# Seven half-size products in place of eight for 18 of 22 gate and up pairs of a SwiGLU layer

## Chip, cores and metric

The kernel runs on one core of one Trainium2 chip. The metric is the device time of one execution in microseconds; for a version it is the median of its runs. The profile is one more execution, taken by the hardware profiler.

## The reference, cut to what matters

```
x = x + 0.5 * swiglu(rms_norm(x), gate1, up1, down1)
x = x + mixer(rms_norm(x))        # GLA, differential attention, short convolution
x = x + 0.5 * swiglu(rms_norm(x), gate2, up2, down2)
return rms_norm(x)
swiglu(h, Wg, Wu, Wd) = (silu(h @ Wg) * (h @ Wu)) @ Wd
```

x is 512 tokens by 1024, in float32. Wg and Wu are 1024 by 2816, Wd is 2816 by 1024. The change touches the two SwiGLU layers only.

## The kernel before

**Numbers in two parts.** Every large product is made of float32 operands that are split in two: a high part rounded to the matmul type fp32r (ScalarE, an ACTIVATE Copy) and the rest (VectorE, a subtraction). `three` (L384) issues three matmuls for one 128 by 128 block of weights: high·high, high weights by low x, low weights by high x. The weights are the stationary operand, the tokens the moving one, so one matmul has 512 columns.

**Slabs.** Weights come in slabs of 128 by 1024 (down: 128 by 1408), numbered through the whole kernel. SyncE loads slab s into `raw[slot s % 2]` when the slab before the last has been split (`load`, L276). `split_hi` (L795, ScalarE) writes `w_hi` once TensorE has used the slab two before (`slab_used`), `split_lo` (L1088, VectorE) writes `w_lo` and counts `lo_ready`, on which TensorE waits (`wait_slab`, L381).

**Up stage** (`ffn_up`, L447 on TensorE, L845 on ScalarE, L1122 on VectorE). 22 pairs, each a gate tile and an up tile of 128 of the 2816 columns: 8 blocks deep, so 24 matmuls of 512 columns for the gate tile, 24 for the up tile. For each pair VectorE scales the gate tile out of PSUM by the inverse norm (L1146), then the up tile (L1150), ScalarE takes silu (L868), VectorE multiplies (L1155), ScalarE makes `h_hi` (L872), VectorE `h_lo` (L1157). In between, both engines split the next slabs. Each engine works its list strictly in the order written.

**Down stage** (`ffn_down`, L479, L885, L1175). Eight output tiles, each 22 blocks deep, two slabs a tile, 66 matmuls of 512 columns; VectorE adds the tile to x (L1172), and the split operand of the next stage is made from it (L807, L1100). GpSimd sums the squares of x for the next norm (L332, L334). In the second layer the last tile is computed in two token halves with matmuls of 256 columns (`last_tile`, L522), so that the final norm of the first half runs beside the second half.

**Start.** The first pair runs as its weights arrive in pieces; the norm of the first layer is ready during the second pair (`mean_squares`, `spread_rms`). Then TensorE makes small products for the mixer (`start_products`, L393) and VectorE their copies (`start`, L1249).

Of the kernel before, what the change touches and what calls it, by code (L numbers as in the profile page):

```python
# [117 lines left out]
def slab_width(s):  # L118

    if s < DN1 or WO <= s < DN2:  # L120
        return UPW
# [1502 lines left out]
```

## Time and profile before

| what | value |
|---|---|
| median of 3 runs | 1024.68 us (1023.26 to 1025.01) |
| the profiled execution, its own time | 1024.96 us |
| its span, first to last instruction | 1023.0 us |
| granted TensorE clock, mean share of full | 0.988 |
| TensorE busy | 1002.9 us of the span (98%) |
| VectorE busy | 500.9 us (49%) |
| ScalarE busy | 356.3 us (35%) |
| GpSimd busy | 73.4 us (7%) |

A matmul's record is longer than the distance to the next one, because matmuls overlap in the array; what a matmul costs in a stream is the distance between two starts. The waits listed with an instruction are the idle time of its engine just before it and the instruction that ended it. A stretch row gives the busy time of each engine between two times.

### The profile page before, as it was taken

Reading aid. Unit: us, or ns where it says so; the run is one execution under the profiler, and the core shown is the slowest. Engines: PE = TensorE matmul, PEld = TensorE weight load, DVE = VectorE, ACT = ScalarE, POOL = GpSimd, SP = SyncE. Lnnn points to the kernel's source line nnn. Section 1 sums busy time; section 2 is a strip of 40 time slices with the busy share of each in tenths; the row PEclk is TensorE's granted clock in tenths of the full one; section 3 lists DMA queues with packets and bytes.
Section 4 is the critical chain, followed back from the end, with each engine's and each line's share of the span. In section 5 each row is a group of like instructions: output and inputs, shape, how many; then the busy total and the mean of one; then the engine's idle time right before and its main releaser. Section 6 shows DMA issues by size and latency. Waiting matters only on the chain.

```text
span 1023.0 us, 13402 instructions
## 1 busy us (share of the span) xinstructions
PE 1002.9 (98%) x5064; PEld 835.2 (82%) x5064; DVE 500.9 (49%) x732; ACT 356.3 (35%) x485; POOL 73.4 (7%) x76
## 2 busy tenths in 40 slices
PE   9999999999999999999989999999999999999996
PEld 8788888888888888777878788888888888888886
DVE  6444444444343433866656874444444444523233
ACT  5444334433321213445723233332332332322231
POOL 0000000000021232000112004300000000000002
PEclk9899999999999999999989999999999999999998
DMA  6222322222323224112211112223222223332312
GB/s 196 87 97 96 103 96 89 103 103 97 113 85 113 85 85 151 63 62 68 71 37 63 63 66 99 92 94 103 84 101 103 89 95 103 113 106 85 113 57 82
DMA packets 28321, 94.89 MB, mean 93 GB/s; under 512 B 3856, under 2 KB 7088, under 8 KB 28288
## 3 DMA queue, kind: packets, MB, share of 16 engines
q1 hardware_dynamic: 26096, 90.98, 26.6%
q0 software_dynamic: 896, 2.39, 0.8%
q10 hardware_dynamic: 1296, 1.07, 0.3%
q8 instruction: 22, 0.36, 0.2%
q14 instruction: 11, 0.09, 0.0%
HBM read 92.00 MB, written 2.42 MB: 92 GB/s over the span
## 4 chain that ended last, share of the span: by engine, by line
PE 45%; DVE 3%; ACT 1%; issue 1%; POOL 0%; DVEq 0%; POOLq 0%
PE ps L386 14%; PE ps L387 14%; PE ps L388 14%; DVE x L1227 1%; PE ps L635 1%; DVE e_dec L1335 1%; DVE a_comp L1355 1%; ACT w_hi L803 0%; PE ps L667 0%; PE ps L675 0%; PE ps L605 0%; DVE w_lo L1094 0%; DVE states L1381 0%; PE ps L511 0%; DVE e_dec L1362 0%
## 5 line engine op out<-in xcount | busy, mean ns | idle before, releaser
L386 PE MATMUL ps<-xg_hi,w_hi 128*128 128x512 f32 x840 | 332.2, 395 | 3.0 <-DVE w_lo L1094 2.1
L387 PE MATMUL ps<-xg_lo,w_hi 128*128 128x512 f32 x840 | 328.5, 391 | 0.0
L388 PE MATMUL ps<-xg_hi,w_lo 128*128 128x512 f32 x840 | 328.5, 391 | 0.0
L803 ACT ACTIVATE w_hi<-raw 128x1024 fp32r<-128x1024 f32 (+2 forms) x153 | 172.6, 1128 | 434.7 <-PE ps L388 434.6
L1094 DVE TENSOR_TENSOR w_lo<-raw,w_hi 128x1024 fp32r<-128x1024 f32 (+2 forms) x153 | 204.0, 1334 | 181.1 <-ACT w_hi L803 181.0
L386 PEld LDWEIGHTS ps<-xg_hi,w_hi 128*128 128x128 f32 x840 | 158.7, 189 | 44.4 <-issue 8.7
L388 PEld LDWEIGHTS ps<-xg_hi,w_lo 128*128 128x128 f32 x840 | 158.5, 189 | 33.5
L387 PEld LDWEIGHTS ps<-xg_lo,w_hi 128*128 128x128 f32 x840 | 158.8, 189 | 32.0
L386 PE MATMUL ps<-h_hi,w_hi 128*128 128x512 f32 (+1 forms) x374 | 141.0, 377 | 0.0
L387 PE MATMUL ps<-h_lo,w_hi 128*128 128x512 f32 (+1 forms) x374 | 140.8, 377 | 0.0
L388 PE MATMUL ps<-h_hi,w_lo 128*128 128x512 f32 (+1 forms) x374 | 140.8, 377 | 0.0
L1150 DVE TENSOR_TENSOR up_s<-ps,rinv 128x512 f32<-128x512 f32 x44 | 30.4, 691 | 112.7 <-PE ps L388 112.7
L388 PEld LDWEIGHTS ps<-h_hi,w_lo 128*128 128x128 f32 x374 | 70.4, 188 | 13.0
L387 PEld LDWEIGHTS ps<-h_lo,w_hi 128*128 128x128 f32 x374 | 70.4, 188 | 12.8
L386 PEld LDWEIGHTS ps<-h_hi,w_hi 128*128 128x128 f32 x374 | 70.4, 188 | 12.8
L872 ACT ACTIVATE h_hi<-up_s 128x512 f32 (+1 forms) x44 | 27.8, 632 | 85.4 <-DVE up_s L1155 85.4
L1146 DVE TENSOR_TENSOR gate_s<-ps,rinv 128x512 f32<-128x512 f32 x44 | 30.4, 691 | 41.5 <-PE ps L388 38.5
L1157 DVE TENSOR_TENSOR h_lo<-up_s,h_hi 128x512 f32 (+1 forms) x44 | 30.5, 692 | 38.8 <-ACT h_hi L872 38.8
L1172 DVE SCALAR_TENSOR_TENSOR x<-ps,x 128x512 f32 (+1 forms) x23 | 15.8, 688 | 67.6 <-PE ps L388 67.6
L1100 DVE SCALAR_TENSOR_TENSOR xg_lo<-x,gain,xg_hi 128x512 fp32r<-128x512 f32 (+1 forms) x24 | 26.0, 1092 | 15.7 <-ACT xg_hi L807 15.7
L386 PE MATMUL ps<-w_hi,xg_hi 128*128 128x384 f32 x96 | 33.2, 346 | 0.0
L387 PE MATMUL ps<-w_lo,xg_hi 128*128 128x384 f32 x96 | 32.7, 341 | 0.0
(188 smaller groups left out, 802.7 us busy)
## 6 DMA issues: line engine op xcount, KB each, us to landing
raw<-up_w SPq DMA_DIRECT2D x86, 512.0 KB, 3.2
raw<-down_w SPq DMA_DIRECT2D x32, 704.0 KB, 4.0
raw<-t_w SPq DMA_DIRECT2D x18, 512.0 KB, 3.2
raw<-out_w SPq DMA_DIRECT2D x8, 512.0 KB, 3.2
raw<-nat_w SPq DMA_DIRECT2D x6, 576.0 KB, 3.8
x<-xT SPq DMA_DIRECT2D x8, 256.0 KB, 6.1
out<-x SPq DMA_DIRECT2D x8, 256.0 KB, 2.2
raw<-nat_w SPq DMA_DIRECT2D x3, 384.0 KB, 3.2
```

What stands on the lines that cost most here:

```text
L386: pe.matmul(out_ap, a[0], b[0], start=first, stop=False)
L387: pe.matmul(out_ap, a[0], b[1], start=False, stop=False)
L388: return pe.matmul(out_ap, a[1], b[0], start=False, stop=last)
L635: last = pe.matmul(ps[c * CHUNK:(c + 1) * CHUNK, bank + hd, col + b * CHUNK:col + (b + 1) * CHUNK], a, bb, start=True, stop=True)
L803: act.activation(w_hi[:, slot(s), 0:w], raw[:, slot(s), 0:w], ACT.Copy).then_inc(hi_ready, 1)
L872: act.activation(h_hi[:, m, :], up_s[:, b, :], ACT.Copy).then_inc(h_hi_ready, 1)
L1094: dve.tensor_tensor(w_lo[:, slot(s), 0:w], raw[:, slot(s), 0:w], w_hi[:, slot(s), 0:w], ALU.subtract).then_inc(lo_ready, 1)
L1100: dve.scalar_tensor_tensor(xg_lo[:, k, :], x[:, k, :], gain[:, gi, bass.ds(k, 1)], xg_hi[:, k, :], ALU.mult, ALU.subtract).then_inc(xg_lo_ ...
L1146: dve.tensor_tensor(gate_s[:, b, :], ps[:, b, :], rinv[:], ALU.mult).then_inc(gate_scaled, 1)
L1150: dve.tensor_tensor(up_s[:, b, :], ps[:, 2 + b, :], rinv[:], ALU.mult).then_inc(up_scaled, 1)
L1157: dve.tensor_tensor(h_lo[:, m, :], up_s[:, b, :], h_hi[:, m, :], ALU.subtract)\
L1172: dve.scalar_tensor_tensor(x[:, k, :], ps[:, bank, :], scale, x[:, k, :], ALU.mult, ALU.add)\
```

## The change

Of the 22 pairs of each layer the first four (`PLAIN`) stay as they are. The other 18 (`FAST`) are called units here. A unit is a product of [weights: two halves of the depth × (gate, up)] with [x: two halves of the depth × two halves of the tokens]. It is computed by Winograd's form of Strassen's scheme: seven products M1 to M7 of half the depth (4 blocks) and 256 tokens, each 4 × 3 = 12 matmuls of 256 columns, in place of eight such quarters (48 matmuls of 512 columns).

- The products need sums of the operands. Those of x (S1 to S4) are made once a layer, during the plain pairs: `a1` on ScalarE, `s_operands` on VectorE, then the split `s_hi` and `s_lo`.
- Those of the weights (T1 to T4) are made for every unit: T1 and T3 on GpSimd (`sums`), T2 and T4 on VectorE (`t2`, `t4`); they and the up slab's second half (U2) are split in three groups, GA = T1, T2; GB = T3; GC = T4, U2. Only the gate slab is still split as a slab; the up slab goes to a buffer of its own, `raw_u`.
- Results are combined on the way out of PSUM: `take` copies a partial sum to `snap` on ScalarE, and c11, c21, c12, c22 on VectorE make the four quarters (256 columns each). Banks A, B and C exist twice.
- The up tile is no longer scaled by the norm; `tile` in the down stage scales the result instead (two instructions for one), `last_half` likewise.
- h is kept in float32 and split into `h_hi` and `h_lo` in the down stage (`split_h`), where the tiles are now computed in pairs with 22 slabs of 1024 columns in place of 16 of 1408.
- The small start products move: `start_lambda` behind pair 2, `start_bias` behind unit 1, `start` behind unit 1 on VectorE. GpSimd's sums stand in its queue ahead of the store of the bias table.

The core of the diff, in the order SyncE, GpSimd, TensorE, ScalarE, VectorE. i and b number the units, v = 2i + b; f is the layer.

```diff
+def load_unit(f, up0, b, i):
+    v = 2 * i + b
+    s = up0 + 2 * PLAIN + b
+    load(s, up_w[f, v + PLAIN, 0], 2 * i)
+    if isinstance(i, int) and i == 0:
+        sp.wait_ge(slab_used, up0 + 2)
+    else:
+        sp.wait_ge(gc_lo, v + (FAST * f - 1))
+    sp.dma_start(raw_u[:, b, :], up_w[f, v + PLAIN, 1]).then_inc(u_loaded[b], 16)
...
+def sums(f, up0, b, i):
+    v = 2 * i + b
+    s = up0 + 2 * PLAIN + b
+    pool.wait_ge(raw_loaded[slot(s)], 16 * i + loads(s))
+    pool.wait_ge(u_loaded[b], 16 * i + 16 * (FAST // 2 * f + 1))
+    if not (isinstance(i, int) and v + f == 0):
+        pool.wait_ge(ga_lo, v + FAST * f)
+    pool.tensor_tensor(t_raw[:, T1, :], raw[:, slot(s), 0:HW], raw_u[:, b, 0:HW], ALU.add)\
+        .then_inc(t1_ready, 1)
+    if not (isinstance(i, int) and v + f == 0):
+        pool.wait_ge(gb_lo, v + FAST * f)
+    pool.tensor_tensor(t_raw[:, T3, :], raw_u[:, b, 0:HW], raw_u[:, b, HW:UPW], ALU.add)\
+        .then_inc(t3_ready, 1)
...
+    def blocks(bank, moving, hi, lo, first):
+        for j in range(HK):
+            c = slice(j * P, (j + 1) * P)
+            end = three(ps[:, bank, 0:HALF], (hi[:, c], lo[:, c]), moving[j],
+                        first and j == 0, j == HK - 1, not first)
+        return end
...
+    def m1_m2(i, b):
+        v = 2 * i + b
+        s = up0 + 2 * PLAIN + b
+        g_hi, g_lo = w_hi[:, slot(s), :], w_lo[:, slot(s), :]
+        if isinstance(i, int) and i == 0:
+            pe.wait_ge(gate_scaled, PLAIN * f + PLAIN - 1 + b)
+        else:
+            pe.wait_ge(c21_scaled, v + (FAST * f - 1))
+        wait_slab(s, 2 * i)
+        blocks(A_BANK[b], x_block(0, 0), g_hi[:, 0:HW], g_lo[:, 0:HW], True).then_inc(m1_done, 1)
+        if not (isinstance(i, int) and i == 0):
+            pe.wait_ge(c11_added, v + (FAST * f - 1))
+        blocks(C_BANK[b], x_block(HK, 0), g_hi[:, HW:UPW], g_lo[:, HW:UPW], True)\
+            .then_inc(slab_used, 1)
+    def m4_m3(i, b):
+        v = 2 * i + b
+        pe.wait_ge(gc_lo, v + (FAST * f + 1))
+        pe.wait_ge(snap_ready[2], v + (FAST * f + 1))
+        blocks(A_BANK[b], x_block(HK, 1), sum_hi[:, T4, :], sum_lo[:, T4, :], False)\
+            .then_inc(m4_done, 1)
+        pe.wait_ge(c22_done, v + (FAST * f + 1))
+        blocks(B_BANK[b], s_block(S4), sum_hi[:, U2, :], sum_lo[:, U2, :], False)\
+            .then_inc(m3_done, 1)
+    def m6_m5_m7(i, b):
+        v = 2 * i + b
+        if isinstance(i, int) and v == 0:
+            pe.wait_ge(s_lo_ready, HK * (f + 1))
+        pe.wait_ge(ga_lo, v + (FAST * f + 1))
+        pe.wait_ge(snap_ready[0], v + (FAST * f + 1))
+        blocks(A_BANK[b], s_block(S2), sum_hi[:, T2, :], sum_lo[:, T2, :], False)\
+            .then_inc(m6_done, 1)
+        if isinstance(i, int) and i == 0:
+            pe.wait_ge(h_ready, FT * f + PLAIN - 1 + b)
+        else:
+            pe.wait_ge(c12_done, v + (FAST * f - 1))
+        blocks(B_BANK[b], s_block(S1), sum_hi[:, T1, :], sum_lo[:, T1, :], True)\
+            .then_inc(m5_done, 1)
+        pe.wait_ge(gb_lo, v + (FAST * f + 1))
+        pe.wait_ge(snap_ready[1], v + (FAST * f + 1))
+        blocks(A_BANK[b], s_block(S3), sum_hi[:, T3, :], sum_lo[:, T3, :], False)\
+            .then_inc(m7_done, 1)
...
+    for m in range(1, PLAIN):
+        pair(m)
+        if f == 0 and m == 2:
+            start_lambda()
+    m1_m2(0, 0)
+    m6_m5_m7(0, 0)
+    m1_m2(0, 1)
+    m4_m3(0, 0)
+    m6_m5_m7(0, 1)
     if f == 0:
-        start_products()
-    with pe.Fori(1, FT // 2) as i:
-        for b in range(2):
-            pair(i, b)
+        start_bias()
+    with pe.Fori(1, FAST // 2) as i:
+        m1_m2(i, 0)
+        m4_m3(i - 1, 1)
+        m6_m5_m7(i, 0)
+        m1_m2(i, 1)
+        m4_m3(i, 0)
+        m6_m5_m7(i, 1)
+    m4_m3(FAST // 2 - 1, 1)
...
+        for i, (m, kk) in enumerate(down_tiles(d)):
+            if q == 0 and m == 0:
+                pe.wait_ge(h_lo_ready, FT * f + kk + 1)
+            last = three(ps[:, DOWN_BANKS[q % 2][m % 2], :], part(dn0 + d, i * P, (i + 1) * P),
+                         (h_hi[kk], h_lo[:, kk, :]), kk == 0, kk == FT - 1)
...
+        if m == 0:
+            for j in range(HK):
+                act.activation(a1[:, j, :], x[:, j, :], ACT.Copy, scale=gain[:, gi, j:j + 1])\
+                    .then_inc(a1_ready, 1)
+        if m == 1:
+            act.wait_ge(s_made, HK * (f + 1))
+            for j in range(HK):
+                act.activation(s_hi[:, j, :, :], s_raw[:, j, :, :], ACT.Copy).then_inc(s_hi_ready, 1)
+        if m == PLAIN - 1:
+            ga(0, 0)
+            gb(0, 0)
...
+    def take(q, i, b, bank, done, used):
+        v = 2 * i + b
+        act.wait_ge(done, v + (FAST * f + 1))
+        if not (isinstance(i, int) and v + f == 0):
+            act.wait_ge(used, v + FAST * f)
+        act.activation(snap[:, q, :], ps[:, bank[b], 0:HALF], ACT.Copy).then_inc(snap_ready[q], 1)
+    def silu(i, b):
+        v = 2 * i + b
+        act.wait_ge(c11_scaled, v + (FAST * f + 1))
+        act.wait_ge(c21_scaled, v + (FAST * f + 1))
...
+    def unit(i, b, prev):
+        v = 2 * i + b
+        s = up0 + 2 * PLAIN + b
+        if prev:
+            take(2, *prev, A_BANK, m7_done, c22_done)
+            gb(i, b)
+        take(0, i, b, A_BANK, m1_done, c11_added)
+        if prev and isinstance(i, int) and v == FAST - 1:
+            split_hi(s + 2 * i + 1)
+        else:
+            split_hi(s + 1, 2 * i)
+        if prev:
+            silu(*prev)
+            act.wait_ge(m3_done, v + FAST * f)
+        act.wait_ge(t4_ready, v + (FAST * f + 1))
+        act.activation(sum_hi[:, GC, :], raw_u[:, b, :].rearrange("p (a c) -> p a c", a=2), ACT.Copy)\
+            .then_inc(gc_hi, 1)
+        take(1, i, b, A_BANK, m6_done, c12_done)
+        if not (isinstance(i, int) and v == FAST - 1):
+            ga(*((i, 1) if b == 0 else (i + 1, 0)))
...
+    def s_operands():
+        for j in range(HK):
+            dve.wait_ge(a1_ready, HK * f + j + 1)
+            dve.scalar_tensor_tensor(s_raw[:, j, S1, :], x[:, HK + j, HALF:S], gain[:, gi, HK + j:HK + j + 1],
+                                     a1[:, j, HALF:S], ALU.mult, ALU.subtract).then_inc(s_diff, 1)
+        dve.tensor_tensor(s_raw[:, :, S3, :], a1[:, :, 0:HALF], a1[:, :, HALF:S], ALU.subtract)
+        dve.wait_ge(s_diff, (HK + 1) * f + HK)
+        dve.scalar_tensor_tensor(s_raw[:, :, S2, :], s_raw[:, :, S1, :], -1.0, a1[:, :, 0:HALF],
+                                 ALU.mult, ALU.subtract).then_inc(s_diff, 1)
+        dve.wait_ge(s_diff, (HK + 1) * (f + 1))
+        for j in range(HK):
+            dve.scalar_tensor_tensor(s_raw[:, j, S4, :], x[:, HK + j, 0:HALF],
+                                     neg_gain[:, gi, HK + j:HK + j + 1], s_raw[:, j, S2, :],
+                                     ALU.mult, ALU.subtract).then_inc(s_made, 1)
...
+        if m == PLAIN - 1:
+            t2(0, 0)
+            t4(0, 0)
+        if m:
+            split_lo(s + 2)
+        if m == PLAIN - 1:
+            ga(0, 0)
+            gb(0, 0)
+        dve.wait_ge(slab_used, s + 2)
+        dve.wait_ge(silu_done, FT * f + m + 1)
+        dve.tensor_tensor(h[:, m, :], gate_s[:, b, :], ps[:, 2 + b, :], ALU.mult).then_inc(h_ready, 1)
+        if m and m < PLAIN - 1:
+            split_lo(s + 3)
+        if m == 1:
+            s_operands()
+        if m == 2:
+            for j in range(HK):
+                dve.wait_ge(s_hi_ready, HK * f + j + 1)
+                dve.tensor_tensor(s_lo[:, j, :, :], s_raw[:, j, :, :], s_hi[:, j, :, :], ALU.subtract)\
+                    .then_inc(s_lo_ready, 1)
+    def t2(i, b):
+        v = 2 * i + b
+        dve.wait_ge(t1_ready, v + (FAST * f + 1))
+        dve.tensor_tensor(t_raw[:, T2, :], t_raw[:, T1, :], raw_u[:, b, HW:UPW], ALU.add)\
+            .then_inc(t2_ready, 1)
+    def t4(i, b):
+        v = 2 * i + b
+        dve.wait_ge(t3_ready, v + (FAST * f + 1))
+        dve.wait_ge(t2_ready, v + (FAST * f + 1))
+        dve.tensor_tensor(raw_u[:, b, 0:HW], t_raw[:, T2, :], raw[:, slot(up0 + 2 * PLAIN + b), HW:UPW],
+                          ALU.add).then_inc(t4_ready, 1)
...
+    def ga(i, b):
+        dve.wait_ge(ga_hi, 2 * i + b + (FAST * f + 1))
+        dve.tensor_tensor(sum_lo[:, GA, :], t_raw[:, GA, :], sum_hi[:, GA, :], ALU.subtract)\
+            .then_inc(ga_lo, 1)
...
+    def gc(i, b):
+        dve.wait_ge(gc_hi, 2 * i + b + (FAST * f + 1))
+        dve.tensor_tensor(sum_lo[:, GC, :], raw_u[:, b, :].rearrange("p (a c) -> p a c", a=2),
+                          sum_hi[:, GC, :], ALU.subtract).then_inc(gc_lo, 1)
+    def c22(i, b):
+        v = 2 * i + b
+        dve.wait_ge(snap_ready[2], v + (FAST * f + 1))
+        dve.scalar_tensor_tensor(h[:, PLAIN + v, HALF:S], ps[:, B_BANK[b], 0:HALF], -1.0, snap[:, 2, :],
+                                 ALU.mult, ALU.subtract).then_inc(c22_done, 1)
...
+    def unit(i, b, prev, following):
+        v = 2 * i + b
+        s = up0 + 2 * PLAIN + b
+        if prev:
+            c22(*prev)
+            ga(i, b)
+            gb(i, b)
+        dve.wait_ge(snap_ready[0], v + (FAST * f + 1))
+        dve.wait_ge(slab_used, 2 * i + (s + 1))
+        dve.tensor_tensor(gate_s[:, b, 0:HALF], ps[:, C_BANK[b], 0:HALF], snap[:, 0, :], ALU.add)\
+            .then_inc(c11_added, 1)
+        if following:
+            t2(*following)
+        dve.wait_ge(c11_added, v + (FAST * f + 1))
+        dve.tensor_tensor(gate_s[:, b, 0:HALF], gate_s[:, b, 0:HALF], rinv[:, 0:HALF], ALU.mult)\
+            .then_inc(c11_scaled, 1)
+        if prev:
+            c21(*prev)
+            c12(*prev)
+        gc(i, b)
+        if following:
+            t4(*following)
+        if prev:
+            gated(*prev)
+        if following:
+            split_lo(s + 1, 2 * i)
+        else:
+            split_lo(s + 2 * i + 1)
...
+    c22(last, 1)
+    split_h(f, 0)
+    split_h(f, 1)
+    c21(last, 1)
+    c12(last, 1)
+    split_lo(up0 + 2 * PLAIN + FAST + 1)
+    gated(last, 1)
...
+def split_h(f, kk):
+    dve.wait_ge(h_hi_ready, FT * f + kk + 1)
+    dve.tensor_tensor(h_lo[:, kk, :], h[:, kk, :], h_hi[kk], ALU.subtract).then_inc(h_lo_ready, 1)
...
+    def tile(m, used):
+        q, b = divmod(m, 2)
+        dve.wait_ge(slab_used, dn0 + used)
+        dve.scalar_tensor_tensor(gate_s[:, b, :], ps[:, DOWN_BANKS[q % 2][b], :], 0.5, rinv[:],
+                                 ALU.mult, ALU.mult).then_inc(down_scaled, 1)
+        dve.wait_ge(down_scaled, KT * f + m + 1)
+        dve.tensor_tensor(x[:, m, :], x[:, m, :], gate_s[:, b, :], ALU.add).then_inc(x_updated, 1)
```

## Rows read from the trace of the kernel before

**Rows 1.** The page: busy time of the engines, and one line of its loads.
```profile
PE 1002.9 (98%) x5064; PEld 835.2 (82%) x5064; DVE 500.9 (49%) x732; ACT 356.3 (35%) x485; POOL 73.4 (7%) x76
...
raw<-up_w SPq DMA_DIRECT2D x86, 512.0 KB, 3.2
```

**Rows 2.** Stretch, its length, busy us (instructions) of PE, PEld, DVE, ACT, POOL, clock, DMA.
```profile
700.00:800.00 100.00, 100.00 (x443) 82.84 (x442) 47.82 (x56) 30.90 (x38) 0.00 (x0) 1.00 0.28 94
```

**Rows 3.** TensorE in order of time, 994 to 996: start us, us, engine, line.
```profile
994.66 0.28 PE L386 MATMUL ps<-h_hi,w_hi 128*128 128x256 f32 x1
...
995.98 0.28 PE L388 MATMUL ps<-h_hi,w_lo 128*128 128x256 f32 x1
```

**Rows 4.** VectorE in order of time, second up stage and the end.
```profile
661.83 1.23 DVE L1094 TENSOR_TENSOR w_lo<-raw,w_hi 128x1024 fp32r<-128x1024 f32 x1 [4.60 <-ACT w_hi L803]
662.98 0.68 DVE L1146 TENSOR_TENSOR gate_s<-ps,rinv 128x512 f32<-128x512 f32 x1
663.58 0.68 DVE L1150 TENSOR_TENSOR up_s<-ps,rinv 128x512 f32<-128x512 f32 x1
...
672.54 0.69 DVE L1150 TENSOR_TENSOR up_s<-ps,rinv 128x512 f32<-128x512 f32 x1 [3.12 <-PE ps L388]
...
1012.17 0.41 DVE L1214 SCALAR_TENSOR_TENSOR x<-ps,x 128x256 f32<-128x256 f32 x1
```

**Rows 5.** ScalarE in order of time, around the openings of both up stages.
```profile
32.47 0.63 ACT L868 ACTIVATE gate_s<-gate_s 128x512 f32<-128x512 f32 x1
...
34.39 1.04 ACT L803 ACTIVATE w_hi<-raw 128x1024 fp32r<-128x1024 f32 x1
...
651.05 0.72 ACT L807 ACTIVATE xg_hi<-x,gain 128x512 fp32r<-128x512 f32 x1 [1.89 <-DVE x L1172]
...
667.10 1.06 ACT L803 ACTIVATE w_hi<-raw 128x1024 fp32r<-128x1024 f32 x1 [1.38 <-PE ps L388]
668.07 0.61 ACT L868 ACTIVATE gate_s<-gate_s 128x512 f32<-128x512 f32 x1
...
1008.43 0.38 ACT L831 ACTIVATE rinv<-ps 128x256 f32<-128x256 f32 x1 [3.16 <-PE ps L518]
```

**Rows 6.** Hand-overs in the up stage: TensorE to VectorE, ScalarE to VectorE.
```profile
153.72 0.39 PE L388 MATMUL ps<-xg_hi,w_lo 128*128 128x512 f32 x1
...
154.15 0.69 DVE L1146 TENSOR_TENSOR gate_s<-ps,rinv 128x512 f32<-128x512 f32 x1 [0.91 <-PE ps L388]
...
155.52 1.06 ACT L803 ACTIVATE w_hi<-raw 128x1024 fp32r<-128x1024 f32 x1
...
156.61 1.23 DVE L1094 TENSOR_TENSOR w_lo<-raw,w_hi 128x1024 fp32r<-128x1024 f32 x1 [1.77 <-ACT w_hi L803]
...
165.03 0.69 DVE L1146 TENSOR_TENSOR gate_s<-ps,rinv 128x512 f32<-128x512 f32 x1 [0.91 <-PE ps L388]
```

**Rows 7.** The opening of the first up stage: last split, then TensorE.
```profile
35.73 1.22 DVE L1094 TENSOR_TENSOR w_lo<-raw,w_hi 128x1024 fp32r<-128x1024 f32 x1
...
37.00 0.79 PE L386 MATMUL ps<-xg_hi,w_hi 128*128 128x512 f32 x1 [2.15 <-DVE w_lo L1094]
...
37.59 0.63 PE L387 MATMUL ps<-xg_lo,w_hi 128*128 128x512 f32 x1
```

**Rows 8.** The stretch after that restart, columns as in rows 2.
```profile
36.90:42.10 5.20, 5.10 (x12) 4.04 (x13) 4.44 (x12) 2.60 (x4) 0.00 (x0) 0.50 0.58 195
```

**Rows 9.** GpSimd and VectorE at the same time, first down stage.
```profile
303.47 1.04 POOL L332 TENSOR_TENSOR sq<-x 128x512 f32 x1 [11.38 <-DVE x L1172]
...
303.81 2.18 DVE L1094 TENSOR_TENSOR w_lo<-raw,w_hi 128x1408 fp32r<-128x1408 f32 x1 [0.60 <-ACT w_hi L803]
...
304.59 2.56 POOL L334 TENSOR_TENSOR sq_sum<-sq_sum,sq 128x512 f32<-128x512 f32 x1
...
305.91 1.78 DVE L1100 SCALAR_TENSOR_TENSOR xg_lo<-x,gain,xg_hi  x1
...
311.36 1.62 DVE L1094 TENSOR_TENSOR w_lo<-raw,w_hi 128x1408 fp32r<-128x1408 f32 x1 [3.67 <-ACT w_hi L803]
```

More of the change, by code:

```diff
@@ new lines, in s_block @@
+                def s_block(q):
+                    return [(s_hi[:, j, q, :], s_lo[:, j, q, :]) for j in range(HK)]
+                def m1_m2(i, b):
[12 more added lines that the diff above has]
+                        .then_inc(slab_used, 1)
@@ L845, in ffn_up @@
             def ffn_up(f, up0):
[L846 to L860 removed]
+                gi = 2 * f
@@ new lines, in ffn_up @@
+                for m in range(PLAIN):
+                    pair(m)
+                    if f == 0 and m == 2:
+                        act.wait_ge(start_mm, 1)
+                        act.activation(lam[:, 0:2], ps[:, 7, 0:2], ACT.Exp, scale=float(D)).then_inc(start_act, 1)
+                unit(0, 0, None)
+                unit(0, 1, (0, 0))
+                with act.Fori(1, FAST // 2 - 1) as i:
+                    unit(i, 0, (i - 1, 1))
+                    unit(i, 1, (i, 0))
+                last = FAST // 2 - 1
@@ new lines, in ffn_up @@
+                unit(last, 0, (last - 1, 1))
+                unit(last, 1, (last, 0))
+                take(2, last, 1, A_BANK, m7_done, c22_done)
+            def split_h(f, kk):
+                if kk == 0:
+                    act.wait_ge(gc_lo, FAST * (f + 1) - 1)
+                if kk == 2:
+                    act.wait_ge(ga_lo, FAST * (f + 1))
+                if kk == 4:
+                    act.wait_ge(gc_lo, FAST * (f + 1))
+                if kk == 6:
+                    act.wait_ge(m3_done, FAST * (f + 1))
+                act.wait_ge(h_ready, FT * f + kk + 1)
+                act.activation(h_hi[kk], h[:, kk, :], ACT.Copy).then_inc(h_hi_ready, 1)
@@ L1162, in ffn_up @@
+                for m in range(PLAIN):
+                    pair(m)
+                unit(0, 0, None, (0, 1))
+                unit(0, 1, (0, 0), (1, 0))
                 if f == 0:
                     start()
-                with dve.Fori(1, FT // 2 - 1) as i:
-                    for b in range(2):
-                        pair(i, b)
-                for b in range(2):
-                    pair(FT // 2 - 1, b)
+                with dve.Fori(1, FAST // 2 - 1) as i:
+                    unit(i, 0, (i - 1, 1), (i, 1))
+                    unit(i, 1, (i, 0), (i + 1, 0))
```

459 lines of the change are left out of this document (266 added, 193 removed).

## The prediction

> **What bounds the kernel now.** I read the page first: TensorE is busy for 98% of the span, VectorE for 49%, ScalarE for 35% [rows 1]. Then the stretches: in the up stage TensorE is busy for 100.00 of 100 us at full clock, with VectorE at 48 and ScalarE at 31 [rows 2]. Then the order of time, for the distance between matmuls. One pair takes 165.03 - 154.15 = 10.88 us, gate copy to gate copy [rows 6]: 48 x 0.2267 us. So TensorE alone sets the time, and what TensorE is spared is saved, as long as the other engines keep up. What is to be checked is the time of one unit.
>
> **TensorE's part.** The last tile already uses 256 columns, reloading the weights for every matmul: 11 distances take 995.98 - 994.66 = 1.32 us, 0.120 each [rows 3]. A product M is 12 x 0.120 = 1.44 us; a unit is 84 x 0.120 = 10.08. That saves 0.80 us a unit, 36 x 0.80 = 28.8 us, if TensorE never waits. The count falls by an eighth, the time by 7.4%, since each matmul carries about 13 ns beside its columns (2 x 0.120 - 0.2267). The Trainium skill (TensorE: Matmul & The Clock Gate, Back-to-back issue gap) has N/2.4 + 2.5 ns: 109 and 216 ns, which would save 1.19 us a unit; the trace does not agree, and its 120 and 227 ns decide.
>
> **Prices of the others.** VectorE: 1024 columns 1.23 us, 512 columns 0.69, 256 columns 0.41; the next one that need not wait starts 0.08 before the end (662.98 - 661.83 = 1.15, 663.58 - 662.98 = 0.60) [rows 4]. ScalarE: 1.06, silu of 512 0.62, 0.38 for 256 out of PSUM, 0.72 with a gain [rows 5]; it starts its next one 0.10 early. Hand-overs: a matmul's result is seen 0.43 us after its start at 512 columns (0.39 + 0.04) [rows 6], so 0.28 + 0.04 = 0.32 at 256 [rows 3]; ScalarE to VectorE 0.03 [rows 6]; VectorE to TensorE 0.05 (36.95 to 37.00), and a restarted TensorE loses another 0.16 at half clock (0.59 against 0.43) [rows 7], say 0.08 at full clock. VectorE's twelve instructions of a unit are 3 x 1.23 + 4 x 0.69 + 5 x 0.41 = 8.5 us against 5.2 for a pair. That is below 10.08, so the order decides.
>
> **The unit's chain.** TensorE's order is M1, M2 of v, M4, M3 of v-1, M6, M5, M7 of v. M3 of v-1 ends 4 x 1.44 = 5.76 us after M1 starts; its last matmul starts at 5.64 and is seen at 5.96. Only then may ScalarE overwrite the high part of GC (its wait on m3_done, since M3 reads it): 5.96 + 1.06 = 7.02. VectorE, strictly in order: gc at 7.05, t4 at 8.20, gated at 8.80, and last the gate slab of the next unit, 9.40 + 1.23 = 10.63. On this M1 of the next unit waits: 10.68, or 10.76 with the restart. TensorE would be ready at 10.08. So 0.6 to 0.7 of the 0.80 us is given back as a new wait ahead of each M1.
>
> **VectorE's own round** is as long. From c22 at 0: ga 0.33, gb 1.48 to 2.17. GpSimd's T1 for the next unit waits for ga; what its adds cost beside VectorE the down stage shows. Its 128x512 product took 1.04 us; a subtraction of VectorE that began inside it lasted 2.18 against 1.62 with GpSimd idle; GpSimd's next one lasted 2.56, ending 1.16 after that subtraction [rows 9]. The two take turns. So T1 ends at 2.17 + 1.16 = 3.33 and T3, waiting for nothing, at 4.45. VectorE makes c11 meanwhile (its input is in PSUM), and t2 ends about 0.54 after T3, at 4.99, as an instruction held up had ended 0.54 after GpSimd's (307.69 against 307.15) [rows 9]. Then c11's scaling to 5.3, c21 to 5.65, silu 5.78 to 6.40, ScalarE's GC to 7.37, gc at 7.40, t4 8.55, gated 9.15, split 9.75 to 10.98, the next c22 at 10.9. The two bounds are 10.7 and 10.9; I take 10.85, nearer the longer. 36 x (10.85 - 10.88) = -1 us. The up slab's load starts behind gc of v-2 and needs about 3.2 us [rows 1], between 8.6 in one round and T1 at 2.2 in the next: 4.5 us, hidden, with 1 us to spare.
>
> **Openings, first layer.** (a) ScalarE makes a1 (4 x 0.62 = 2.5 us) behind the silu of 32.47, where h_hi (0.6) and table loads stood; the split of 34.39 [rows 5] starts near 35.5, VectorE's ends at 37.8 in place of 36.95, and TensorE waits 0.8 longer. (b) In pair 2 VectorE's s_lo (4 x 1.15) meets two sums of GpSimd (+2.3): TensorE, restarted at 37.85 with 12 matmuls at half clock, ends pair 2 at 51.3; h and the split of pair 3's up slab bring VectorE to 53.7, s_lo then runs to 60.6; gate copy, t2, t4 and the split of unit 0's gate slab end near 63.6, TensorE is ready at 62.4: 1.2. (c) start_bias and start stand behind unit 1, with no slack there: TensorE about 1.3, then VectorE's copies; 2.0 in all, where they now lie under an existing wait. **Second layer.** (d) s_operands follows the split of up slab 1: 4 x 0.35 + 1.15 + 1.2 + 4 x 0.35 = 5.2 us. With the up tile read at 672.54 [rows 4] it ends at 680.0; ScalarE's s_hi takes four times 1.0 to 684.0; only behind it stands the split of pair 3's gate slab: ScalarE to 685.1, VectorE to 686.3. TensorE wants it 10.88 us after 672.3, at 683.2: a wait of 3.1. (In the first layer the late start covers this.) (e) As (b): 0.9. **Into the down stage**, each layer: (f) behind unit 17 VectorE makes c22, two h_lo, c21, c12, a slab, gated, and then the third h_lo, 7.0 us after M7; TensorE has done M4, M3 (2.88) and two blocks of h (2.72) at 5.6: 1.45. Later, one h_lo is 0.60 us and TensorE uses 1.36 for each: hidden under the first pair of tiles, in whose 132 x 0.2267 = 30 us the 22 x 0.60 fit. **End**: (g) one more instruction in last_half, 0.45. Sum: 0.8 + 1.2 + 2.0 + 1.45 = 5.45; 3.1 + 0.9 + 1.45 = 5.45; 0.45; 11.35 us. The down stage's matmuls, 66 a tile, stay.
>
> **The clock.** After the wait of 2.15 us, 12 matmuls ran at half clock, 0.43 us each [rows 7, 8]: 12 x 0.2 = 2.4 us lost. Today this happens once in an up stage; (a) keeps it. (d) is a longer wait, so I add 2.4 there; bounds 0 and 2.4 for each of (b) to (f). Waits of 0.7 us inside units I price at nothing: 93% of the time is matmuls.
>
> **Sum** against the profiled execution's own 1024.96: -1 + 11.35 + 2.4 = 1037.7. The median of the runs lies 0.28 lower: **1037 us**.
>
> **Rivals.**
> *TensorE stays the bound.* The place is the stretch from the end of M3 of v-1 to the next M1: TensorE needs three products, 4.32 us, for which the chain above needs 4.92. If it is under 4.32, a unit is 10.08, the waits of the openings stay: 1024.7 + 13.8 - 28.8 = 1009.7, faster than before. For it: VectorE has 1.5 us less work than a unit lasts. Against: every term is a row, and they add up to 0.6 too much. 13%.
> *The chain holds, the openings are hidden.* 36 x (10.68 - 10.88) = -7, and of the 13.8 only some 4 remain: 1021 to 1025. 15%, half of it faster.
> *GpSimd's second sum falls behind t2.* The Trainium skill (SBUF — State Buffer, two separate sides) says that whichever of the two starts first holds the shared ports for its whole instruction; rows 9 agree. If t2 gets in between T1 and T3, T3 ends near 5.5, c11's scaling waits for it, and all behind moves by 0.45: 11.3 a unit, +16: 1053. Against: GpSimd waits for nothing there, while VectorE must first see T1. 10%.
> *The clock falls at (b), (c) and both (f) too*: 4 x 2.4: 1047. 12%.
> My forecast has 50%.
>
> **How the numbers follow.** Faster by over 0.2% (about what a measurement of this kernel can tell from no change): 13 + 8 = 21; within 0.2%: 6; slower: the rest, 73. The range leaves out most of the first rival below, and the third rival's top: 1018 to 1053.
>
> **What would show it.** In units: gate slab's split last in VectorE's round, a wait of 0.6 to 0.8 us ahead of M1 on that split, c22 to c22 at 10.7 to 10.9; VectorE at 75 to 90% busy, and GpSimd's adds at 1.0 to 1.2 us or stretched to 1.8. A wait of 3 us ahead of pair 3's gate product in the second layer. 256-column matmuls 0.120 apart. It is wrong if TensorE shows no waits in units (first rival), or if T3 ends behind t2.

## The result, and the profile after

The changed kernel takes 1053.82 us (median of 4 runs, 1052.21 to 1055.22) against 1024.76 for the kernel before in the same session: a ratio of 1.0286, 95% interval 1.0265 to 1.0308. It is slower, as forecast, but by 29 us where 12 were expected, and it ends 0.8 us above the top of the range of 1018 to 1053.

Of the profiled execution, first the engines (busy us, share of the span, instructions), which answer to [rows 1]:

```profile
span 1050.8 us, 16633 instructions
PE 987.7 (94%) x6360; PEld 874.8 (83%) x6360; DVE 670.4 (64%) x1038; ACT 438.9 (42%) x680; POOL 172.5 (16%) x148
```

Then TensorE's waits that bear on the change, the largest first (engine, tile and line, what it waited for: us in total, times, the longest):

```profile
PE ps L481 <- DVE w_lo L1350: 37.0, 38, 4.6
PE ps L481 <- DVE xg_lo L1350: 3.1, 1, 3.1
...
PE ps L507 <- POOL sq_sum L404: 2.3, 2, 2.1
PE ps L481 <- ACT snap L1070: 1.8, 3, 0.7
...
PE ps L481 <- DVE h_lo L1538: 1.6, 4, 0.5
```

TensorE has 15 us less work than before (1002.9 to 987.7), and idles 63 us in place of 20. The first line is mostly the wait ahead of M1 in the units. One whole unit, and three stretches of 6 us that begin within 0.3 us of a long wait's end (span of the stretch, busy us and instructions of each engine, granted clock, DMA share, GB/s):

```profile
171.70:182.70 11.00, 10.20 (x84) 10.00 (x84) 8.59 (x13) 5.36 (x9) 2.93 (x2) 1.00 0.29 101
395.00:401.00 6.00, 5.76 (x27) 5.76 (x28) 2.06 (x6) 0.27 (x1) 6.00 (x13) 0.72 0.71 191
699.30:705.30 6.00, 5.92 (x19) 4.76 (x20) 6.00 (x6) 0.14 (x1) 1.51 (x1) 0.72 0.84 323
1021.50:1027.50 6.00, 5.98 (x28) 5.98 (x29) 2.82 (x4) 1.35 (x2) 0.00 (x0) 0.50 0.00 0
```

A unit of 11 us holds the 84 matmuls, at full clock, and about 0.8 us in which TensorE stands. From the first matmul of a stage to that of the next, after less before: start +0.2, first up stage +4.6, first down stage +4.8, the mixer's first slabs +4.0, the rest of mixer and output -1.0, second up stage +6.4, second down stage +1.6, the last tile to the end +7.1. Before rounding that is 27.8, the difference of the spans.

Inside a unit, in order of time: VectorE, ScalarE and GpSimd (start, duration, engine, line, and in brackets the idle time just before and what ended it), and then TensorE's wait:

```profile
164.01 0.42 DVE L1495 TENSOR_TENSOR gate_s<-ps,snap 128x256 f32<-128x256 f32 x1 [1.22 <-PE ps L483]
164.35 1.40 DVE L1432 TENSOR_TENSOR t_raw<-t_raw,raw_u 128x512 f32<-128x512 f32 x1
165.67 0.41 DVE L1500 TENSOR_TENSOR gate_s<-gate_s,rinv 128x256 f32<-128x256 f32 x1
166.01 0.41 DVE L1468 TENSOR_TENSOR gate_s<-ps,rinv 128x256 f32<-128x256 f32 x1
...
168.13 1.23 DVE L1455 TENSOR_TENSOR sum_lo<-raw_u,sum_hi 128x1024 fp32r<-128x1024 f32 x1 [0.83 <-ACT sum_hi L1094]
169.27 0.68 DVE L1440 TENSOR_TENSOR raw_u<-t_raw,raw 128x512 f32<-128x512 f32 x1
169.87 0.69 DVE L1482 TENSOR_TENSOR h<-h,gate_s 128x512 f32 x1
170.47 1.22 DVE L1350 TENSOR_TENSOR w_lo<-raw,w_hi 128x1024 fp32r<-128x1024 f32 x1
...
166.51 0.63 ACT L1076 ACTIVATE gate_s<-gate_s 128x512 f32<-128x512 f32 x1 [2.67 <-DVE gate_s L1468]
167.05 1.04 ACT L1094 ACTIVATE sum_hi<-raw_u 128x1024 fp32r<-128x1024 f32 x1
...
162.27 1.68 POOL L425 TENSOR_TENSOR t_raw<-raw,raw_u 128x512 f32<-128x512 f32 x1 [8.03 <-DVE sum_lo L1445]
163.91 1.28 POOL L429 TENSOR_TENSOR t_raw<-raw_u 128x512 f32<-128x512 f32 x1
...
171.74 0.39 PE L481 MATMUL ps<-xg_hi,w_hi 128*128 128x256 f32 x1 [0.78 <-DVE w_lo L1350]
```

Read it from below: M1 at 171.74 waits for the split of 170.47, the last in VectorE's row of gc (168.13), t4, the product for h (`gated`) and the split. gc waits for ScalarE's high part of GC (167.05), which stands behind the silu of 166.51, which waits for VectorE's C21 (166.01, a quarter of the result), which stands in VectorE's queue behind t2 (164.35). And t2, 0.68 us of work, lasts 1.40, since GpSimd's T3 ran from 163.91 to 165.19. From C11's add to C11's add the steady units take 10.98 us, 10.88 and 11.09 in turn.

The end of the run shows the part that the forecast lacks. VectorE, then TensorE, at the last tile:

```profile
1012.58 1.22 DVE L1350 TENSOR_TENSOR xg_lo<-raw,xg_hi 128x1024 fp32r<-128x1024 f32 x1 [4.69 <-ACT xg_hi L977]
1013.72 0.68 DVE L1551 SCALAR_TENSOR_TENSOR gate_s<-ps,rinv 128x512 f32<-128x512 f32 x1
...
1016.44 0.68 DVE L1551 SCALAR_TENSOR_TENSOR gate_s<-ps,rinv 128x512 f32<-128x512 f32 x1
...
1018.54 0.69 DVE L1366 TENSOR_TENSOR sq_sum<-sq_sum,sq 128x512 f32<-128x512 f32 x1 [0.70 <-ACT sq L987]
1020.24 2.09 DVE L1350 TENSOR_TENSOR xg_lo<-raw,xg_hi 128x1024 fp32r<-128x1024 f32 x2 [1.01 <-ACT xg_hi L977]
...
1021.52 0.58 PE L481 MATMUL ps<-h_hi_s,xg_hi 128*128 128x256 f32 x1 [3.13 <-DVE xg_lo L1350]
```

Two finished tiles (1013.72 and 1016.44, each with its add, square and sum, handed between VectorE and ScalarE) stand between two slab splits. The second split is late, TensorE waits 3.13 us, and the stretch from 1021.50 then runs at half clock. (That the clock fell all the way for 6 us is this execution's: see the last section.)

### The profile page after: what moved, and what is told of

Read it like the earlier page. It is cut to its first block and busy times, and to the rows that moved or that the text cites. A ratio compares the mean times of both kernels' runs of the same rounds, so it can differ in the third digit from the quotient of the medians.

```text
span 1050.8 us, 16633 instructions
## 1 busy us (share of the span) xinstructions
PE 987.7 (94%) x6360; PEld 874.8 (83%) x6360; DVE 670.4 (64%) x1038; ACT 438.9 (42%) x680; POOL 172.5 (16%) x148
## 3 DMA queue, kind: packets, MB, share of 16 engines
q10 hardware_dynamic: 1296, 1.07, 0.3%
## 5 line engine op out<-in xcount | busy, mean ns | idle before, releaser
L1350 DVE TENSOR_TENSOR w_lo<-raw,w_hi 128x1024 fp32r<-128x1024 f32 (+3 forms) x130 | 159.9, 1231 | 179.2 <-ACT w_hi L977 179.2
L481 PE MATMUL ps<-xg_hi,w_hi 128*128 128x256 f32 (+1 forms) x552 | 192.9, 349 | 35.7 <-DVE w_lo L1350 34.7
L977 ACT ACTIVATE w_hi<-raw 128x1024 fp32r<-128x1024 f32 (+3 forms) x130 | 134.1, 1031 | 215.4 <-PE ps L483 215.1
L482 PE MATMUL ps<-xg_lo,w_hi 128*128 128x256 f32 (+1 forms) x552 | 185.5, 336 | 0.0
L483 PE MATMUL ps<-xg_hi,w_lo 128*128 128x256 f32 (+1 forms) x552 | 185.5, 336 | 0.0
L481 PE MATMUL ps<-s_hi,sum_hi 128*128 128x256 f32 x576 | 161.9, 281 | 0.7 <-ACT snap L1070 0.7
L482 PE MATMUL ps<-s_lo,sum_hi 128*128 128x256 f32 x576 | 161.8, 281 | 0.0
L483 PE MATMUL ps<-s_hi,sum_lo 128*128 128x256 f32 x576 | 161.7, 281 | 0.0
L482 PE MATMUL ps<-h_lo,w_hi 128*128 128x512 f32 x330 | 128.5, 389 | 0.0
L481 PEld LDWEIGHTS ps<-s_hi,sum_hi 128*128 128x128 f32 x576 | 110.5, 192 | 0.9 <-issue 0.9
```

Of the source, the lines that this page charges most:

```text
L481: pe.matmul(out_ap, a[0], b[0], start=first, stop=False, skip_group_check=resumed)
L482: pe.matmul(out_ap, a[0], b[1], start=False, stop=False, skip_group_check=resumed)
L483: return pe.matmul(out_ap, a[1], b[0], start=False, stop=last, skip_group_check=resumed)
L977: act.activation(dst, raw[:, slot(s), 0:w], ACT.Copy).then_inc(hi_ready, 1)
L1350: dve.tensor_tensor(lo, raw[:, slot(s), 0:w], hi, ALU.subtract).then_inc(lo_ready, 1)
```

## The experiments

All ratios are against the kernel before, whose median in these sessions was 1023.65 to 1024.13 us.

**1. The finished tiles of the down stage, two slabs earlier.**

```
-q, i = divmod(d, PAIR_SLABS)
-if q and q < KT // 2 and i == 1:
+q, i = divmod(d + 1, PAIR_SLABS)
+if q < KT // 2 and i == 0:
...
-if q == KT // 2 - 1 and i == 4:
+if q == KT // 2 - 1 and i == 3:
```

> Changed kernel, with the finished tiles of the down stage taken two slabs earlier: in the lists of ScalarE and VectorE a pair of tiles is scaled and added right behind the split that its last slab releases, and tile 6 behind the split that its third slab releases, ahead of the next splits. Theory (late tiles): in the changed kernel two tiles' work (about 7 us on VectorE and ScalarE in turn) stands between two splits, while the third slab of tile 6 is only 768 wide, so the next split comes late: TensorE waits 1.84 us at the end of the first down stage, 2.13 us for the sum of squares at the mixer's start, 3.13 us in the last tile with half clock behind it. Expected: these three waits gone or under 0.5 us, 1041 to 1046 us. Rival (narrow slab): two splits fall due within the 4.1 us of the 768-wide slab whatever stands between them, so the waits stay near 2 and 3 us, 1051 to 1054 us.

Measured: 1043.89 us, 1.0201 [1.0181, 1.0222], 9.9 us less than the changed kernel, as the theory had it. Its last tile, TensorE first, and then a window from there:

```profile
1017.77 0.38 PE L481 MATMUL ps<-h_hi_s,xg_hi 128*128 128x256 f32 x1 [1.13 <-DVE xg_lo L1350]
```

```profile
1017.77:1023.77 6.00, 5.92 (x48) 5.74 (x49) 1.50 (x5) 1.19 (x3) 0.00 (x0) 1.00 0.01 3
```

The wait falls from 3.13 to 1.13 us, and 48 matmuls fit into 6 us where 28 did. The wait at the mixer's first sum falls from 2.13 to 0.70, and the clock there stays full. The one of 1.84 at the end of the first down stage is gone. Two of the three waits so stay above the 0.5 us that the theory allowed; what makes the rest was not tried (the narrow slab, the rival, may have its part in it).

By stages of the two profiled executions, the first down stage is 1.9 us shorter, the mixer's first slabs 3.0, the part from the last tile on 5.0. The rest of the mixer is 1.4 longer. The second up stage, where nothing was edited, is 1.4 shorter: behind the same wait of 3.32 us the clock stayed full this time.

**2. The gate slab's split ahead of gc.** The loads of the unit's slab wait for t4 as well, which reads the buffer.

```
+if following:
+    split_lo(s + 1, 2 * i)
...
 gc(i, b)
 if following:
     t4(*following)
 if prev:
     gated(*prev)
-if following:
-    split_lo(s + 1, 2 * i)
```

> Changed kernel, with VectorE's split of the next gate slab moved within the unit, from last (behind gc, t4, gated) to ahead of gc; the load of the gate slab waits for t4 instead of the split. Same instructions. Theory (chain): each unit waits for M3, ScalarE's high part of GC, VectorE's gc, t4, gated and the gate slab's split, and the split is now free of it: the wait of 0.8 us ahead of M1 goes, a unit takes 10.08 to 10.25 us in place of 10.98, 36 units give 26 to 32 us: 1022 to 1028 us. Rival (VectorE's own round with GpSimd's turns is what lasts 10.9): the wait moves to another semaphore, a unit stays at 10.7 or more, 1044 to 1052 us.

Measured: 1033.63 us, 1.0086 [1.0064, 1.0108]; 20.2 us less, 6 to 12 short of the theory. The wait ahead of M1 is gone, a unit takes 10.30 us, where 10.08 to 10.25 were expected. 36 units give 36 x 0.68 = 24.5 us, and new waits in the first units take some back: 3.30 us at unit 1 of the first layer (half clock behind it), where VectorE's t2 waits 3.54 us for T1 and its transfer, and 0.76 and 1.15 in the second. Here VectorE, GpSimd and SyncE's issues in one unit:

```profile
148.77 1.23 DVE L1459 TENSOR_TENSOR sum_lo<-raw_u,sum_hi 128x1024 fp32r<-128x1024 f32 x1 [0.24 <-ACT sum_hi L1098]
...
154.88 1.77 DVE L1436 TENSOR_TENSOR t_raw<-t_raw,raw_u 128x512 f32<-128x512 f32 x1 [0.69 <-POOL t_raw L429]
...
157.57 1.21 DVE L1354 TENSOR_TENSOR w_lo<-raw,w_hi 128x1024 fp32r<-128x1024 f32 x1
159.03 1.23 DVE L1459 TENSOR_TENSOR sum_lo<-raw_u,sum_hi 128x1024 fp32r<-128x1024 f32 x1 [0.25 <-ACT sum_hi L1098]
...
153.56 1.28 POOL L429 TENSOR_TENSOR t_raw<-raw,raw_u 128x512 f32<-128x512 f32 x1 [7.72 <-DMA raw_u<-up_w]
...
150.16 0.33 SPq L349 DMA_DIRECT2D raw_u<-up_w  x1
```

A new loop holds the unit, and a transfer is in it: gc ends at 150.00 and frees the up half's buffer; SyncE issues at 150.16; GpSimd's T1 starts at 153.56 when the half has landed; VectorE waits for it 0.69 us and is then held 1.77 us in t2 beside T3; behind t2 in its queue stand C11's scaling, C21, C12, the split (157.57) and the next gc (159.03). 159.03 - 148.77 = 10.26 us. The prediction gave this transfer 1 us to spare; the split in front of gc takes 1.2.

**3. The high parts of s behind the split of pair 3's gate slab** (ScalarE; from `m == 1` to `m == 2`, after `split_hi(s + 2)`).

> Changed kernel, with ScalarE's four high parts of the token sums (s_hi) moved from the end of pair 1 to behind the split of pair 3's gate slab in pair 2. Theory: the wait of 3.3 us ahead of pair 3 in the second layer, and the half clock behind it, go; in the first layer 0.5 us. 1047 to 1050 us. Rival: VectorE's sums (s_operands) alone make the split late, the wait only shrinks to 1 us or moves to unit 0, where s_lo now ends later: 1051 to 1054 us.

Measured: 1050.01 us, 1.0265 [1.0243, 1.0287], 3.8 us less. The wait of 3.32 us ahead of pair 3 in the second layer is gone, but one of 2.85 stands ahead of unit 0, for the split (707.82) that now comes behind the later low parts of s (699.08 to 705.91):

```profile
709.19 0.36 PE L481 MATMUL ps<-xg_hi,w_hi 128*128 128x256 f32 x1 [2.85 <-DVE w_lo L1350]
```

So the wait moved, as the rival has it, though the time is the theory's. Little of the 3.8 us can be put down to the edit: of the 3.0 us between the two profiled executions only 0.7 lies in the second up stage (5.75 us over before, where it was 6.44), and the first up stage is 0.3 longer. 1.8 lies from the last tile on, which the edit does not touch and where TensorE waits the same 3.1 us: the clock behind it was 0.72 of full over 6 us here and 0.50 in the changed kernel.

**4. GpSimd's two sums on 8 of 512 columns**, in all units but the first (the rest of T1 and T3 is left out).

> Changed kernel, with GpSimd's two weight sums of a unit made on 8 of 512 columns only, but for the first unit of each layer (the sums T1 and T3 are left out, the output is not the reference's). Theory (chain through M3 and ScalarE): GpSimd's turns lengthen only VectorE's part ahead of c21, which lies beside TensorE's M3, so a unit falls from 10.98 to 10.75 to 10.85 us and the wait ahead of M1 stays over 0.5 us: 1045 to 1049 us. Rival (GpSimd holds the ports, the bound is VectorE's round): a unit falls to 10.1 to 10.4 us: 1025 to 1033 us.

Measured, one run: 1040.29 us, between the two ranges. A unit takes 10.71 us (10.64 and 10.78 in turn), just under the theory's 10.75, and the wait ahead of M1 is 0.51: the chain through M3 that the prediction put at 10.68 to 10.76. ScalarE's high part of GC now waits for TensorE's M3, where in the changed kernel it stood behind the silu without waiting:

```profile
152.42 1.06 ACT L1095 ACTIVATE sum_hi<-raw_u 128x1024 fp32r<-128x1024 f32 x1 [0.26 <-PE ps L484]
```

What GpSimd's turns cost is the other 0.27 us a unit, 9.7 us in all. Of the rest of the difference, 2.0 us lie from the last tile on, where the clock was again 0.72 in place of 0.50.

**5. The same on top of the early split.**

> The early split of the gate slab alone, and GpSimd's two sums on 8 of 512 columns in all units but the first (that kernel's products of these units are then of partly stale sums). Theory (with the split early, TensorE bounds a unit at 84 x 0.120 = 10.1 us and GpSimd's turns on VectorE's path are covered): the unit goes from 10.30 to 10.15 to 10.30 us, the kernel 1029 to 1034. Rival (GpSimd's turns still set the small waits on the copies of partial sums): the unit at 10.10 and the kernel at 1024 to 1028.

Measured, one run: 1016.3 us, the unit 9.94: beyond the rival. So the early split's unit is set by the loop of T1 and t2; with T1 and T3 short, and t2 not held up, TensorE does not wait at all in the steady units, and its own unit is 9.94 / 84 = 0.1183 us a matmul.

**6. The first three together.**

> The finished tiles two slabs earlier, the gate slab's split ahead of gc, and the high parts of s behind the split of pair 3's gate slab, all at once. Theory (three separate stalls, at three places that do not touch): the gains measured one by one against the changed kernel add up: 9.9 + 20.2 + 3.8 = 33.9 us, so 1053.8 - 33.9 = 1019.9, range 1018 to 1023; the waits of 3.30 us at unit 1 and of 1.15 us in layer 2 that the early split brought stay. Rival (the stalls cover one another: with one gone, the next engine in line is late by as much): 1024 to 1032, and the windows of the units show a wait ahead of most products again.

Measured: 1030.61 us, 1.0063 [1.0048, 1.0079], in the rival's range. The gains do not add. The units are at 10.50 us where the early split alone had 10.30, which is 7 of the missing 11: the loop of experiment 2 moves with its transfer, and VectorE's wait for T1 in the steady units is 0.95 us in the mean (0.62 to 1.34) where it was 0.73 (0.44 to 1.22). Why the same units waited longer for the same transfers was not settled. The other 4 us need no new stall: from the last tile on, the three single kernels were 5.0, 1.9 and 1.8 us shorter in their profiled executions than the changed kernel, and all of them together can give only the 4.9 that they give here. Two of the three gains at that place were the clock's and no edit's.

**7. The second sum for unit 2 behind gc, in unit 1 alone.**

```
-if following:
+if following and not (isinstance(i, int) and i == 0 and b == 1):
     t2(*following)
```

> As the one with all three, and in unit 1 of both layers VectorE's second sum for unit 2 stands behind the split and gc, not ahead of the scaling of C11. Theory (the 3.30 us before the third block of unit 1 in layer 1, and the 1.15 us in layer 2, are VectorE standing 3.5 us in that sum while the slab's up half for unit 2 is still under way, with C11's scaling, C21, C12 and the next silu queued behind): 3 to 5 us less than the kernel with all three, so 1015 to 1017. Rival (the wait is the ScalarE table or TensorE's bias products beside it): within 1 us of the kernel with all three.

Measured: 1024.87 us, 1.0008 [0.9999, 1.0018]: 5.7 us less than experiment 6, somewhat more than the 3 to 5 of the theory; its 1015 to 1017 was counted from the 1019.9 that experiment 6 did not reach. The waits of 2.65 and 1.88 us at unit 1 are gone, waits of 1.24 and 0.62 stand at unit 2. Experiment 9 does the same in every unit.

**8. The low parts of s in two halves.**

> As the one before, and the low parts of s in two halves: tiles 0 and 1 behind pair 2's up half, tiles 2 and 3 behind pair 3's split and sums. Theory (with the high parts of s moved, the four low parts, 6.8 us beside GpSimd's first sums, hold pair 3's gate scaling and the split of the first unit's slab by some 1 to 1.5 us in each layer): 1 to 3 us less again, 1012 to 1016. Rival (low parts are needed by the third product of unit 0 and their second half is late there instead): no change, or 1 us more.

Measured: 1023.93 us, 1.0006 [0.9994, 1.0017]; no difference from the one before that these intervals can tell, which is the rival. In the second layer the wait of 1.45 us ahead of unit 0 is gone, and one of 1.07 us at its third product has taken its place.

**9. The second sum behind gc in every unit, split early.**

```
-if following:
-    t2(*following)
 dve.wait_ge(c11_added, v + (FAST * f + 1))
...
 gc(i, b)
 if following:
+    t2(*following)
     t4(*following)
```

> The early split of the gate slab alone, and VectorE's second sum for the next unit behind the split and gc in every unit. Theory (with the split early a unit runs in a loop that holds a transfer: gc of unit v frees its up half's buffer, the 512 KB transfer takes 3.3 us, GpSimd's first sum 1.3, VectorE's second sum stands held 1.8 beside GpSimd's next one, and behind it in VectorE's queue stand C11's scaling, C21, C12, the split and the next gc: 10.3 us together): taken out of that queue, the sum has 3 us to spare, a unit falls from 10.30 to 9.95 to 10.1 us, TensorE's own, and the kernel from 1033.6 to 1020 to 1025. Rival (VectorE itself has no time left beside GpSimd's turns, 8.9 us of work in 10.3): the unit stays above 10.2 and the kernel at 1029 or more.

Measured: 1018.62 us, 0.9944 [0.9927, 0.9960], 1.4 us below the theory's range; 15.0 us less than with the early split alone. One unit, and VectorE and GpSimd in it:

```profile
171.70:181.65 9.95, 9.95 (x86) 9.95 (x86) 8.49 (x13) 5.27 (x8) 3.11 (x2) 1.00 0.35 105
```

```profile
171.48 0.69 DVE L1436 TENSOR_TENSOR t_raw<-t_raw,raw_u 128x512 f32<-128x512 f32 x1
...
175.34 1.67 POOL L429 TENSOR_TENSOR t_raw<-raw,raw_u 128x512 f32<-128x512 f32 x1 [6.84 <-DVE sum_lo L1449]
176.97 1.48 POOL L433 TENSOR_TENSOR t_raw<-raw_u 128x512 f32<-128x512 f32 x1
```

TensorE is busy for 9.95 of 9.95 us. T1 waits for ga again (L1449), not for the transfer; t2 lasts 0.69, with nothing of GpSimd beside it. GpSimd's sums still take turns with VectorE (1.67 us for T1, against 1.28 in experiment 2), and it costs TensorE nothing.

**10. The same edit with the split left last.**

> The changed kernel with the second sum behind gc in every unit and nothing else: the gate slab's split stays last. Theory (here the unit's loop is the one through M3, ScalarE's high part of GC, gc, t4, the product for h, the split and M1; the second sum, 0.6 us, now stands in that loop, and what it was held up before stood outside it): the unit goes from 10.98 to 11.2 to 11.6 us, the kernel from 1053.8 to 1060 to 1073, though the same edit took 15 us off with the split early. Rival (the second sum's wait for GpSimd is the cost in either order): 1030 to 1045.

Measured: 1068.42 us, 1.0432 [1.0413, 1.0452], the theory: the unit is 11.50 us. TensorE's wait ahead of M1 grows from 0.8 to 1.3 us. One and the same move of a 0.69 us instruction is worth -15.0 us in one order and +14.6 in the other.

**11. All of it together**: tiles early, split early, the parts of s moved, the second sum behind gc.

> The tiles two slabs earlier, the early split, both halves of the moved parts of s, and VectorE's second sum behind gc in every unit. Theory: a unit of 9.95 to 10.1 us in place of 10.47, so 1023.9 - 31 x 0.4 = about 1011, range 1008 to 1015. Rival (the sum, now late, delays the high parts of GA and so the third product): 1019 to 1025.

Measured: 1004.81 us, 0.9817 [0.9801, 0.9833]: 6 us below the theory's figure, which took 31 units at 0.4 us; the 36 units fell from about 10.47 to 9.94, and 36 x 0.53 = 19 us is what was measured (1023.9 - 1004.8).

**12. And ScalarE's products of x with the gain, in layer 1, behind both splits of pair 1.**

```
-if m == 0:
+if m == 1 - f:
     for j in range(HK):
         act.activation(a1[:, j, :], x[:, j, :], ACT.Copy, scale=gain[:, gi, j:j + 1])
```

> As the one before, and in layer 1 ScalarE's four products of x with the gain, 2.54 us, behind both splits of pair 1 in place of ahead of them. Theory (they stand ahead of the split of pair 2's first slab, which TensorE waits for): 1.0 to 1.5 us less, 1007 to 1013. Rival (the parts of s are then late at pair 3 or at unit 0): no change.

Measured: 1001.07 us (5 runs, 999.26 to 1003.66), 0.9780 [0.9762, 0.9798]: faster than both kernels. It is 3.7 us below the one before it, where 1.0 to 1.5 were expected: TensorE's first long wait is 2.50 us in place of 4.63 (2.1 us, more than the theory's 1.5), and the 15 matmuls behind it run at full clock, where the kernel before had half [rows 8] and experiment 11 had 7 in 3 us at 0.50. The window from that wait's end:

```profile
35.66:39.00 3.34, 3.34 (x15) 2.77 (x16) 3.30 (x7) 2.79 (x5) 0.00 (x0) 1.00 0.59 212
```

Its span and engines:

```profile
span 997.5 us, 16622 instructions
PE 971.4 (97%) x6360; PEld 866.4 (87%) x6360; DVE 668.4 (67%) x1038; ACT 438.4 (44%) x680; POOL 179.2 (18%) x148
```

## Why the prediction was right in direction and short in size

**TensorE's part** held. A product's matmul was put at 0.120 us [rows 3]; it takes 0.1183 (experiment 5). Experiment 9 shows all of the gain: 9.95 us a unit against 10.88.

**The unit's chain and VectorE's round** were the right two bounds, and the longer one decides. The chain was put at 10.68 to 10.76 and measured 10.71, with GpSimd out of the way. VectorE's round was put at 10.9, T3 before t2 as forecast, and measured 10.98. The forecast took 10.85, between them; a unit obeys the longer. The term was mis-sized by 0.13 us, 36 x 0.13 = 4.7 us. That the two bounds lie 0.27 us apart is measured too; a forecast between them could only come out right by luck.

**The openings** came out near their terms in size, not all in place. (a) 0.8 against 38.12 - 37.00 = 1.1. (b) 1.2 ahead of unit 0 against waits of 0.51 ahead of pair 3 and 0.57 ahead of unit 1. (c) 2.0 against 0.69 and 1.62, of which some 0.8 is the wait that every unit has. (d) 3.1 against 3.32, and the clock fell there, as forecast (in experiment 1, behind the same wait, it did not). (e) 0.9 ahead of unit 0 against 0.30 and 1.08 ahead of units 1 and 2, of which again some 0.8 is every unit's. (f) 1.45 against 0.56, 0.48 and 0.29. The clock stayed full at (b), (c), (e) and (f). Both up stages with the start were forecast at 9.4 us together, of which -1 for the units, and measured 11.3. That is closer than the terms are: the units cost 4.7 us more than forecast, and the openings less.

**The step that failed** is "The down stage's matmuls, 66 a tile, stay". The matmuls do; what stands around them does not. The change works on two tiles at once, so they finish together; each costs VectorE two instructions where one stood; and they are taken up behind a split, so that the two tiles' work, which VectorE and ScalarE hand to and fro, lies between two splits. Costed at nothing, this is 4.8 - 1.45 = 3.4 us in the first down stage (a wait of 1.84 among them), 3.0 in the mixer (GpSimd's squares late, a wait of 2.13 and then a lowered clock), and 7.1 - 0.45 = 6.6 at the last tile (3.13, and half clock behind it): 13.0 us. With 1.9 in the up stages and 0.2 in the second down stage that is the missing 15.1. Experiment 1 moves the tiles alone, and in these stages 8.4 of the 13.0 come back (1.9, then 3.0 less 1.4, then 5.0). Some 1.8 of the 6.6 at the last tile is how far the clock fell in this one execution: six other kernels with the late tiles and the same wait of 3.13 us there were 5.2 to 6.2 us over before from the last tile on, not 7.1. How much of the rest is the pairs and how much the second instruction was not measured apart.

**The rivals.** TensorE as the bound (9.95 a unit) is not what this order gives, but what experiment 9 gives. GpSimd's second sum stayed ahead of t2. The clock fell not where that rival had it, but at the two late places of the down stage.

**The Trainium skill's** rule on the shared ports (SBUF — State Buffer, two separate sides) was the right one to weigh: t2 lasts 1.38 to 1.77 us beside a sum of GpSimd and 0.69 without. In the changed kernel GpSimd's turns are worth 0.27 us a unit (experiment 4). With the early split 0.35 us a unit lies between 10.30 and 9.95, but that is not the price of the ports alone: experiment 5 shortens T1 as well, and experiment 9 also takes VectorE's wait for the transfer out of the loop. In both orders what was lost is the time of the work queued behind t2: C11's scaling, C21, and what waits for them.

## What to carry to other kernels

In a unit that two engines share closely, write down every loop that comes back to its own start, those through a buffer's release and a transfer too, and move first the instruction that another engine can hold up: behind the work that others wait for, not ahead of it. An edit's worth has no sign of its own; the same move was worth -15 and +15 us by which loop was the longest. And where a change lets pieces of work finish in pairs, look at what stands between the transfers and splits of the next slabs, even where the matmuls stay as they were. Last, compare two kernels stage by stage before an edit is given the difference of their totals: experiments 1 and 3 changed by 1.4 and 1.8 us in stages that they left alone.

## What was not expected of the hardware

The granted clock after a wait does not follow from the wait's length alone. In the changed kernel it was full behind waits of 1.62 and 1.84 us and fell to half behind 2.13, 3.13, 3.32 and 4.63; but in the last kernel it was full behind one of 2.50 us, at the place where the kernel before had half clock behind 2.15 [rows 7, 8], and in experiment 6 it was lowered (0.70 over 3 us) behind one of 1.88.

Nor is it the same behind the same wait. Ahead of pair 3 in the second layer TensorE waits 3.32 us in the changed kernel and in experiments 1 and 2; over the next 6 us the clock was 0.72, 1.00 and 0.52 of full. At the last tile, behind 3.13 us, it was 0.50 in the changed kernel and 0.72 in experiments 2 to 5, 9 and 10. Here experiment 1 ahead of pair 3, and experiment 3 at the last tile:

```profile
696.09:702.09 6.00, 6.00 (x27) 4.96 (x28) 6.00 (x6) 0.32 (x2) 1.39 (x1) 1.00 0.85 307
```

```profile
1020.28:1026.28 6.00, 6.00 (x37) 6.00 (x38) 2.81 (x4) 1.35 (x2) 0.00 (x0) 0.72 0.00 0
```

The price is large: at the last tile 28 matmuls in 6 us at 1.2 GHz against 48 at 2.4 GHz, 2.4 us for these 20 on top of the wait of 3.13. A 256-column matmul whose weights change each time took 0.1183 us over whole units, steadily, for 84 in a row.
